# Gate/up weights of experts 2 to 15 in loads of 4 MB with rows of 32 KB, the model columns dealt out four by four, the addition of the expert outputs placed among the gate/up chunks, another seating of the first experts' weights, and the fourth norm in eight banks

## What is computed

```python
def expert_choice_ffn(h, w_router, w_gate, w_up, w_down):
    ...
    top_w, top_idx = lax.top_k(affinity.transpose(0, 2, 1), cap)   # cap = 64 of 512 tokens
    xe = jax.vmap(lambda hb, ib: hb[ib])(h, top_idx)
    hid = jax.nn.silu(jnp.einsum('becd,edf->becf', xe, w_gate)) * jnp.einsum('becd,edf->becf', xe, w_up)
    ye = jnp.einsum('becf,efd->becd', hid, w_down) * top_w[..., None].astype(h.dtype)
    combine = lambda yb, ib: jnp.zeros((S, D), h.dtype).at[ib.reshape(-1)].add(yb.reshape(-1, D))
    ...
# second block, its last part
h = h + swiglu(rmsnorm(h, g_ffn[l]), w_gate[l], w_up[l], w_down[l])
```

## Time and profile before

| | |
|---|---|
| time, median of 3 runs | 2044.65 us (2042.44 to 2046.21) |
| the profiled execution | 2044.67 us, of which the span is 2042.9 us |
| PE / PEld busy | 1902.7 us (93%) / 1124.7 us (55%) |
| DVE / ACT / POOL busy | 693.0 / 466.2 / 26.9 us |
| read from memory | 510.00 MB |
| expert layer, from the first gather to the last addition | about 579 to 1507 us |

### The profile page before, as it was taken

One profiled execution on the slowest core, in us unless ns is written; L12 is line 12 of the kernel. 1 busy time (PEld: TensorE's weight loads), 2 busy tenths in 40 slices (PEclk: granted clock), 3 DMA queues, 4 the chain that ended last, 5 costly groups with the idle time before them and its releaser, 6 DMA issues.

```text
span 2042.9 us, 20340 instructions
## 1 busy us (share of the span) xinstructions
PE 1902.7 (93%) x8656; PEld 1124.7 (55%) x8656; DVE 693.0 (34%) x956; ACT 466.2 (23%) x685; POOL 26.9 (1%) x30
## 2 busy tenths in 40 slices
PE   5989989999979999999998999999999999999998
PEld 5876766556733434343433434342344578888887
DVE  6474465276321021201111121111149732222234
ACT  5347535313201101010100101010131432222223
POOL 0000000000000000000000000000030000000000
PEclk8999989999979999999999999999999999999999
DMA  8212201385579999999999999999971014332211
GB/s 306 83 42 62 62 21 42 124 309 206 236 281 422 428 427 428 427 427 428 426 429 427 428 427 428 427 428 428 416 253 53 30 49 148 104 103 84 102 62 41
DMA packets 102495, 513.41 MB, mean 251 GB/s; under 512 B 5123, under 2 KB 59523, under 8 KB 74371
## 3 DMA queue, kind: packets, MB, share of 16 engines
q1 hardware_dynamic: 98032, 487.93, 59.4%
q10 hardware_dynamic: 4374, 24.18, 3.1%
HBM read 510.00 MB, written 2.10 MB: 251 GB/s over the span
## 4 chain that ended last, share of the span: by engine, by line
PE 70%; DMA 17%; DVE 9%; ACT 3%; issue 1%; POOL 0%; SPq 0%; ACTq 0%; DVEq 0%; POOLq 0%
DMA work<-in_w_exp_up 15%; PE ps L1197 11%; PE ps L1152 10%; PE ps L1362 5%; PE ps L1321 4%; PE ps L1322 4%; PE ps L1323 4%; PE ps L600 3%; PE ps L1075 3%; PE ps L601 3%; PE ps L602 3%; PE ps L584 3%; DVE work L2382 2%; PE ps L1178 2%; PE ps L786 2%
## 5 line engine op out<-in xcount | busy, mean ns | idle before, releaser
L1152 PE MATMUL ps<-work 128*64 128x512 f32 x1280 | 451.8, 607 | 36.1 <-DMA work<-in_w_exp_up 36.1
L1152 PE MATMUL ps<-ring,work 128*64 128x512 f32 x760 | 328.4, 603 | 2.6 <-DMA ring<-in_w_exp_up 2.6
L1152 PEld LDWEIGHTS ps<-work 128*64 128x64 f32 x1280 | 141.0, 140 | 229.6 <-issue 175.0
L2295 DVE TENSOR_TENSOR stay<-stay,ps 64x512 f32<-64x512 f32 x64 | 44.3, 692 | 440.9 <-ACT stay L1734 440.3
L1734 ACT ACTIVATE stay<-ps 64x512 f32<-64x512 f32 x64 | 37.7, 589 | 555.5 <-PE ps L1152 555.5
L1152 PEld LDWEIGHTS ps<-ring,work 128*64 128x64 f32 x760 | 101.5, 139 | 113.1 <-issue 103.6
L1197 PE MATMUL ps<-work 128*64 128x512 f32 x616 | 142.0, 607 | 0.3
L584 PE MATMUL ps<-work,ring 128*128 128x512 f32 x320 | 138.7, 592 | 0.7 <-issue 0.7
L1321 PE MATMUL ps<-xh,wh 128*128 128x512 f32 x352 | 137.0, 389 | 0.0
L1322 PE MATMUL ps<-xl,wh 128*128 128x512 f32 x352 | 136.9, 389 | 0.0
L1323 PE MATMUL ps<-xh,wl 128*128 128x512 f32 x352 | 136.9, 389 | 0.0
(11 more groups left out here) (340 smaller groups left out, 2489.4 us busy)
## 6 DMA issues: line engine op xcount, KB each, us to landing
work<-in_w_exp_up SPq DMA_DIRECT2D x44, 2048.0 KB, 25.6
work<-in_w_exp_down SPq DMA_DIRECT2D x35, 2048.0 KB, 26.4
ring<-in_w_exp_gate SPq DMA_DIRECT2D x30, 2048.0 KB, 24.2
work<-in_w_exp_gate SPq DMA_DIRECT2D x29, 2048.0 KB, 23.9
ring<-in_w_exp_down SPq DMA_DIRECT2D x21, 2048.0 KB, 24.8
ring<-in_w_exp_up SPq DMA_DIRECT2D x15, 2048.0 KB, 23.4
ring<-in_w_in SPq DMA_DIRECT2D x27, 1024.0 KB, 6.7
work<-in_ada_w ACTq DMA_DIRECT2D x16, 1024.0 KB, 6.1
```

The lines of the kernel that those rows point to most:

```text
L1152: i = e.matmul(PS[64 * gu:64 * gu + 64, fb, :], at(XET + 128 * k + 64 * z, 64), weights[:, 512 * fb:512 * fb + 512], start=(k == 0), stop= ...
```

## The change

**Loads and slots.** Expert 1 keeps loads of 2 MB. For experts 2 to 14 gate and up come in four loads of 4 MB (`eg4`, `eu4`, four chunks each, rows of 32 KB) into four places of four slots each (`quads`); even and odd experts swap which two places come first. Down keeps its 2 MB loads, and goes into the two places that chunks 0 to 3 leave. Expert 15 has 4 MB loads for chunks 0 to 3, then 2 MB and 1 MB loads. The first experts' slots are dealt out in another order ("seating"): expert 0's chunk k = 2 now lies in slots 7 and 8, and expert 1's four down loads go to the pairs (7, 8), (22, 6), (4, 5), (9, 10) where they went to (7, 8), (2, 3), (4, 5), (9, 10).

**Columns.** A row of a load now holds four neighbouring columns' weights, also in the smaller loads, and `every_fourth(o, k)`, `raw(o + 512 * (k // 4) + k % 4, [(4, 128)])`, takes the place of `every_second`; the laid-out norm and router weights follow (not shown).

**Addition among the chunks.** `combine(p, tc)` does the two matmuls of one block of 128 tokens and is called behind the chunks k = 2 to 5 of an even expert; DVE's eight `add_back` come ahead of the four products of gate and up.

**Fourth norm.** The transposes use all eight banks, token block by token block, without waiting for `sx_l`; ACT and DVE read `bank(k)`. The dense groups u = 0 and u = 1 run chunk by chunk alternately.

```diff
@@ -132,25 +132,27 @@
-    slots += [13, 14, 11, 12, 15, 16, 7, 8, 2, 3, 4, 5, 9, 10, 21, 0, 1, 19, 20, 22, 6, 13, 14, 11]
-    n = 10
-    for e in range(1, NE):
-        for kk in range(KD // 2):
-            if (e, kk) == (NE - 1, KD // 2 - 1):
-                ex += [("eg", e, 6), ("eu", e, 6), ("eg", e, 7), ("eu", e, 7)]
-                slots += [*pairs[n % 8], *pairs[(n + 1) % 8]]
-            else:
-                ex += [("eg2", e, kk), ("eu2", e, kk)]
-                slots += [pairs[n % 8], pairs[(n + 1) % 8]]
-            n += 2
-        for m in range(4):
-            if e == NE - 1:
-                ex += [("ed", e, 2 * m), ("ed", e, 2 * m + 1)]
-                slots += [*pairs[n % 8]]
-            else:
-                ex += [("ed2", e, m)]
-                slots += [pairs[n % 8]]
-            n += 1
+    slots += [13, 14, 11, 12, 7, 8, 2, 3, 4, 5, 9, 10, 21, 16, 0, 1, 22, 6, 15, 19, 20, 13, 14, 11]
+    for kk in range(KD // 2):
+        ex += [("eg2", 1, kk), ("eu2", 1, kk)]
+        slots += [pairs[(10 + 2 * kk) % 8], pairs[(11 + 2 * kk) % 8]]
+    ex += [("ed2", 1, m) for m in range(4)]
+    slots += [(7, 8), (22, 6), (4, 5), (9, 10)]
+    quads = (((0, 1), (2, 3)), ((11, 12), (13, 14)), ((22, 6), (7, 8)), ((4, 5), (9, 10)))
+    for e in range(2, NE):
+        now, then = (quads[:2], quads[2:])[::1 - 2 * (e % 2)]
+        ex += [("eg4", e, 0), ("eu4", e, 0)]
+        slots += [now[0][0] + now[0][1], now[1][0] + now[1][1]]
+        if e < NE - 1:
+            ex += [("eg4", e, 1), ("eu4", e, 1)]
+            slots += [then[0][0] + then[0][1], then[1][0] + then[1][1]]
+            ex += [("ed2", e, m) for m in range(4)]
+            slots += [*now[0], *now[1]]
+        else:
+            ex += [("eg2", e, 2), ("eu2", e, 2), ("eg", e, 6), ("eu", e, 6), ("eg", e, 7), ("eu", e, 7)]
+            slots += [*then[0], *then[1][0], *then[1][1]]
+            ex += [("ed", e, n) for n in range(8)]
+            slots += [*now[0][0], *now[0][1], *now[1][0], *now[1][1]]
     tail = [("i2", 3), ("i2", 1), ("o2", 0), ("o2", 1)] + [("i2", c) for c in (2, 0, 5, 4)] + [("o2", 2), ("o2", 3)] + [("ff", f) for f in range(33)]
...
@@ -374,11 +382,14 @@
+                r0, a0 = 512 * (key[2] // 2), 2 * (key[2] % 2)
+                return t["w_exp_gate" if kind == "eg2" else "w_exp_up"][key[1], r0:r0 + 512, :].rearrange("(p a) n -> p a n", a=4)[:, a0:a0 + 2, :]
+            if kind in ("eg4", "eu4"):
...
@@ -1085,17 +1100,18 @@
                     i = e.transpose(bank(7, 128, 128 * c), at(OHW + 128 * c, 128), ident)
                 i.then_inc(s["x_ot"], 1)
 
-            def combine(p):
-                e.wait_ge(s["x_oc"], p + 1)
-                e.wait_ge(s["x_ym"], 4 * p + 4)
-                for tc in range(TC):
-                    for dh in range(2):
-                        if tc == 0:
-
-                            e.wait_ge(s["x_hc"], 8 * p + 7 + dh)
-                        else:
-                            e.wait_ge(s["x_ca"], 8 * p + 2 * tc - 1 + dh)
-                        e.matmul(bank(6 + dh), at(OHWT + 128 * tc, 128), at(YE + 512 * dh, 512), start=True, stop=True).then_inc(s["x_cb"], 1)
+            def combine(p, tc):
+                if tc == 0:
+                    e.wait_ge(s["x_oc"], p + 1)
+                    e.wait_ge(s["x_ym"], 4 * p + 4)
+                    e.wait_ge(s["x_xd"], 4 * p + 8)
+                for dh in range(2):
+                    if tc == 0:
+
+                        e.wait_ge(s["x_hc"], 8 * p + 7 + dh)
+                    else:
+                        e.wait_ge(s["x_ca"], 8 * p + 2 * tc - 1 + dh)
+                    e.matmul(bank(6 + dh), at(OHWT + 128 * tc, 128), at(YE + 512 * dh, 512), start=True, stop=True).then_inc(s["x_cb"], 1)
 
             def combine_half(st):
                 if st == 0:
...
@@ -1154,8 +1170,9 @@
-                if z == 0 and p > 0:
-                    combine(p - 1)
+                    if z == 0 and p > 0 and 2 <= k < 6:
+                        combine(p - 1, k - 2)
+
                 if z == 1:
                     if p + 1 < NE // 2:
                         gather(p + 1)
...
@@ -1307,16 +1324,20 @@
                     p.then_inc(s["o2_pe"], 1)
 
             def t4_free(k):
-                if k < 4:
-                    e.wait_ge(s["o2_x"], (7, 8, 3, 4)[k])
-                else:
-                    e.wait_ge(s["sx_l"], SX0 + k - 3)
-            turn(XS4, [0, 1, 2, 3], lambda c: normed(4, c), t4_free, s["t_pe"])
-
-            def dense_3(bk, i, j, each=None):
-                for k in range(KD):
-                    if each is not None:
-                        each(k)
+                e.wait_ge(*((s["o2_x"], 7), (s["o2_x"], 8), (s["o2_x"], 3), (s["o2_x"], 4),
+                            (s["dv"], 4), (s["ln_a"], 1), (s["o2_x"], 5), (s["o2_x"], 6))[k])
+
+            for c in range(TC):
+                e.wait_ge(*normed(4, c))
+                for k in (2, 3, 4, 5, 6, 7, 0, 1) if c == 0 else range(KD):
+                    if c == 0:
+                        t4_free(k)
+                    i = e.transpose(bank(k, 128, 128 * c), at(XS4 + 1024 * c + 128 * k, 128), ident)
+                    if c == TC - 1:
+                        i.then_inc(s["t_pe"], 1)
+
+            def dense_3(bk, i, j, ks=range(KD)):
+                for k in ks:
                     o, x = 256 * k + 128 * j, slice(512 * k, 512 * k + 512)
                     e.matmul(bank(bk), WH[i][:, o:o + 128], XH[:, x], start=(k == 0), stop=False)
                     e.matmul(bank(bk), WH[i][:, o:o + 128], XL[:, x], start=False, stop=False)
...
@@ -1330,12 +1351,20 @@
                         u = 4 * n + 2 * gu + j
                         if j == 0:
                             e.wait_ge(s["fs_l"], FS0 + f + 1)
-                        if u < 4:
-
-                            e.wait_ge(s["sx_l"], SX0 + 5 + u)
-                        else:
+                        if u == 0:
+
+                            for k in range(KD):
+                                e.wait_ge(s["sx_l"], SX0 + k + 1)
+                                p = dense_3(0, 0, 0, [k])
+                                if k > 0:
+                                    dense_3(1, 0, 1, [k - 1])
+                            p.then_inc(s["ff_pe"], 1)
+                            dense_3(1, 0, 1, [KD - 1]).then_inc(s["ff_pe"], 1)
+                        if u < 2:
+                            continue
+                        if u >= 4:
                             e.wait_ge(s["ff_s" if gu == 0 else "ff_m"], 2 * n - 1 + j)
-                        dense_3(2 * gu + j, gu, j, (lambda k: e.wait_ge(s["sx_l"], SX0 + k + 1)) if u == 0 else None).then_inc(s["ff_pe"], 1)
+                        dense_3(2 * gu + j, gu, j).then_inc(s["ff_pe"], 1)
             for n in range(FT // 2):
                 i = n % 2
                 e.wait_ge(s["fs_l"], FS0 + 23 + n)
...
@@ -2289,15 +2318,13 @@
             gathered(0)
             for ex in range(NE):
                 z, p = ex % 2, ex // 2
+                if z == 0 and p > 0:
+                    for n in range(8):
+                        add_back(p - 1, n)
                 for fb in range(4):
                     e.wait_ge(s["x_sl"], 4 * ex + fb + 1)
                     sg = rows(64, 128, SG + 512 * fb, 512)
                     e.tensor_tensor(sg, sg, PS[64:128, fb, :], ALU.mult).then_inc(s["x_hd"], 1)
-                    if z == 0 and p > 0:
-                        add_back(p - 1, fb)
-                if z == 0 and p > 0:
-                    for n in range(4, 8):
-                        add_back(p - 1, n)
                 if z == 1 and p + 1 < NE // 2:
                     gathered(p + 1)
                 if ex == NE - 1:
```

More of the change, by code:

```diff
@@ L218, in build @@
         parts = []
-        for name, start, end in (("stay", 0, HEAD), ("ring", HEAD, WORK), ("work", WORK, AR)):
+        for name, start, end in (("stay", 0, HEAD), ("ring", HEAD, SLOT[4]), ("work", SLOT[4], AR)):
             parts.append((start, end, nc.alloc_sbuf_tensor_at(name, [128, end - start], F32, offset=BASE + 4 * start)))
@@ L401, in rooms_of @@
                 return flat(key)
-            if kind in ("eg2", "eu2", "ed2"):
+            if kind in ("eg2", "eu2"):
+                return twice(key).rearrange("p (a n) -> p a n", a=2)
+            if kind in ("eg4", "eu4"):
+                return four(key)
+            if kind == "ed2":
                 return twice(key)
@@ L436, in last_reader @@
                 return s["wo_pe"], 4 * (key[1] // 2) + 4
[L437 to L438 removed]
+            if kind in ("eg", "eu", "eg2", "eu2", "eg4", "eu4"):
+                k = key[2] if len(kind) == 2 else 2 * key[2] + 1 if kind[2] == "2" else 4 * key[2] + 3
                 return s["x_gu"], 18 * key[1] + (18 if k == KD - 1 else 2 * k + (1 if kind[:2] == "eg" else 2))
```

38 lines of the change are left out of this document (20 added, 18 removed).

## The result

The changed kernel takes 2138.55 us (median of 4 runs, 2136.41 to 2141.7); the kernel before, timed beside it, 2043.55. The ratio is 1.0464, with a 95% interval of 1.0452 to 1.0476: 95 us slower, where 9.4 were predicted and 2062 was the upper end of the range. The direction was right, the size was not. The profiled execution took 2136.41 us, its span is 2134.6.

The account below looks back on a forecast made before the run. The prediction took the streaming of expert weights as the bound up to expert 14's last up load, then TensorE alone. 2044.67 + 11.8 (end of the expert layer) - 2.5 (fourth norm) = 2054.0 us, range 2043 to 2062.

Parts of the forecast that it names:

- The column step: Reading columns four apart instead of two: the same instructions with another step, so 0; bounds nothing and 37 us.
- the four places: Six expert pairs: down loads wait for chunks 0 to 3 and come late; +6.1 us, ends 3.5 and 9.5.
- the addition among the chunks: Even experts' addition inside gate/up: worth 0 by itself, hidden by transfers; without it the four places would starve at each.
- the second rival: Gather in odd experts: reads with a step of four floats take twice the time; 2091 us in all, 4 in 100.
- The longer rows: 54 loads of 4 MB with 32 KB rows save 0.073 us each; -4.0 us, ends 0 and -8.0.
- Expert 1's down loads: The second down load waits for chunk 5 of expert 1 and lands at 662.3 instead of 657.7; +4.6 us.
- they must be issued 2.7 us ahead: Even experts' down loads: issued 2.7 us before the queue's owed transfers end, they keep it full.
- The clock: TensorE behind longer waits for 4 MB loads: a slow stretch in six of ten; 1.0 us at expert 15.
- The end of the layer: Expert 15 starts behind a wait at 1462.0; its gate/up ends at 1491.2, 11.8 us later than 1479.35.
- The fourth norm: With eight banks and two groups by turns, TensorE starts the dense groups at 1673.9; -2.5 us, ends -1.5 and -2.8.

Follow-up runs that it names:

- Experiment 1: The changed kernel with columns read two apart instead of four (weights meet other columns than their own): 2081.33 us, ratio 1.0174.
- experiment 5: The changed kernel with rows of 16 KB in its 4 MB loads and columns two by two: 2078.80 us, ratio 1.0181.
- experiment 10: The changed kernel with 16 KB rows, columns two by two, addition behind gate/up, and expert 1's down loads with (22, 6) last: 2062.31 us, ratio 1.0098.
- experiment 11: The changed kernel with 32 KB rows, columns read two apart, addition behind gate/up, and expert 1's down loads with (22, 6) last: 2063.82 us, ratio 1.0097.
- experiment 8: The kernel of experiment 1 with expert 1's down loads in the order (7, 8), (4, 5), (9, 10), (22, 6): 2076.36 us, ratio 1.0171.
- experiment 2: The kernel before with columns read four apart instead of two, nothing else changed: 2059.72 us, ratio 1.0073.
- experiment 6: The kernel of experiment 1 with the addition of even experts back behind gate/up: 2067.34 us, ratio 1.0123.
- experiment 7: The kernel before with the addition of even experts among their chunks, nothing else changed: 2044.37 us, ratio 1.0003.
- experiment 3: The kernel before with only the change's fourth norm: 2041.76 us, ratio 0.9986.
- the fifth expectation: The text written ahead of experiment 5; its rival had the 16 engines end a 4 MB load up to 1.2 us apart. Measured: 2078.80 us.
- experiment 4: The kernel before with another column step in each expert pair's gather, stationary 1 to 8 floats, once moving 4; only the gathers' times count, 7.4 to 15.5 us.
- experiment 9: The kernel before with further stationary and moving steps in each pair's gather, up to 32 floats; only gather times count, both operands at four 15.38 us.

## Why the prediction was wrong, step by step

Three steps failed. The column step, put at nothing, is 57 of the 84.6 us. In the other 27 are the four places, with the lead that their loads need (some 23 us against 6.1 less 4.0 for the rows), and the addition among the chunks (10 to 14 against 0); the parts were measured in different kernels and do not add exactly.

**"Nothing for the columns four by four: the same instructions, with another step."** This step failed, and with it the weight of the second rival. The instructions are the same, but each pass of the gather takes 15.15 / 64 = 0.237 us instead of 0.121. The argument against the rival compared the gather's passes with transposes that read without a step. In the changed kernel the second norm's transposes read with a step of four, and still follow each other every 0.12 us, as they did with two: so a step of four does not show on them, and they could say nothing of the gather. The trace of before had no step over two, both bounds were written down, and I chose between them by a row that did not bear on it.

**The rival's own price, 37 us, was too low.** Experiment 1 against the changed kernel gives 57. The rival had 7.2 us a pair; it is 130.3 - 122.3 = 8.0 (first pairs), and it left out what lies ahead of expert 3. There the single-column matmuls of the second modulation read with a step of four as well (16 of them 3.5 us instead of 1.8, twice), and the two parts of the gather that lie at expert 0 take 2.3 and 2.8 longer: gate/up of expert 0 starts at 593.4 instead of 586.5, that of expert 2 at 704.5 instead of 687.5.

**The longer rows, -4.0.** Right in the price (9.72 predicted, 9.71 to 9.72 measured), worth nothing in the time (experiments 5 against 1, 10 against 11). That a queue which keeps running dry does not profit from rate is a likely reason, not shown by itself.

**Expert 1's down loads, +4.6.** The mechanism is there: issued at 664.38 behind chunk 5, with the queue dry since 660.5, landed 8.2 us later (7.6 predicted). The queue lost 7.2 us there (6.4 in experiment 1), not 4.6, since it was dry for longer; but part comes back behind it. Its price in the whole is 3.5 to 5 by the medians of experiments 8 and 11, and 0.6 and 5 by their ratios, so not well resolved.

**The four places, +6.1.** Mis-sized. Experiment 11, free of the step, the addition and the gap at expert 1, is 20.3 us over the kernel before, though it has the fourth norm's gain: some 23 for loads of 4 MB into four places. Of these 6.5 are a gap at expert 2 that the prediction did not look at: its second gate load waits until expert 1's down has freed a place, and goes out at 687.9 into a queue dry since 685.2. In the pairs the step that failed is the lead, "they must be issued 2.7 us ahead". That was the price of a start into an empty queue, taken as what a running queue needs. The changed kernel's first down load of expert 3 shows it. It was issued at 779.8, when the load ahead had until 783.2:

```profile
L589 SPq DMA_DIRECT2D work<-in_w_exp_down x1: 327/327/327, 779.8 to 779.8; - x1
...
DMA to landing us min/median/max: 10.3/10.3/10.3
```

It landed at 790.1, not at 783.2 + 4.9 = 788.1, in spite of 3.4 us of lead. Over all expert loads of 2 and 4 MB issued behind 648 us in nine kernels (before, after, experiments 1, 2, 5, 6, 8, 10, 11), with the lead as the landing of the load ahead minus the own issue:

```
lead, us    loads   late by over 0.3   median loss, us
under 1        25          25              4.1
1 to 2         13          13              1.6
2 to 3         38          36              1.8
3 to 4         58          43              0.9
4 to 5         49          17              0.1
5 to 6         50          10              0.1
6 to 8         94           7              0.0
over 8        775          31              0.0
```

So about 6 us of lead are needed for a loss to be rare. The prediction's own leads were 3.2 us at the down loads (1.5 behind a slow stretch) and 2.3 at the next gate load. With experiment 11's leads behind 730 us the prediction's rule, 2.7 less the lead, gives 0.3 us in all, and the queue lost 20.0 (6 in the kernel before); in experiment 1 the rule gives 10.9 of 37.2. The rest of the miss is TensorE, which came later than the sums had it (43.3 against 39.8).

**The clock.** I took six in ten of the longer waits to bring a slow stretch. In the changed kernel all do. Behind the six waits of 6.0 to 7.0 us for the first pair of the experts 3 to 13, 64 passes take 16.3 to 16.9 us, against 13.73 at full clock. Behind the seven waits for the last up load of these experts and the first of expert 15, 62 passes take 15.35 to 16.86 us, against the 13.95 that 62 such passes take in experiment 10 at a granted clock of 1.00. Six of these seven waits are 2.6 to 3.1 us long, no longer than before; the prediction had 4 to 5.7. The window behind the one in expert 3:

```profile
783.30:786.50 3.20, 3.20 (x8) 0.99 (x10) 0.00 (x0) 0.00 (x0) 0.00 (x0) 0.50 0.90 343
```

Of the Trainium skill ("TensorE: Matmul & The Clock Gate", section "HAM oscillation — how this bites in real kernels") it is the rule, weighed in the prediction and set aside in favour of the count over shorter waits, that was borne out in this kernel. It is not so everywhere: in experiment 10, 4 of 13 waits (3.1 to 3.4 us) left the passes at full clock.

**The addition among chunks, 0.** Right for the kernel before (experiment 7), wrong in this one: 10 to 14 us (experiment 6). "Without it the place above would starve" had the sign reversed. It looked at when TensorE finishes, not at when chunk 3 and chunk 7 are read: each block of 1.9 us ahead of a chunk is a block of delay for the loads that wait for its place.

**The end of the layer.** Expert 15 stood behind the wait as foretold, but at 1542.9 instead of 1462, by all of the above. **The fourth norm, -2.5:** right (2.6 in the trace, 2.5 in experiment 3).

Still open is why a load issued 3 to 4 us ahead loses in three of four cases and not in the fourth. Row length is excluded by experiment 5. The traces hold a part of the answer: a load's semaphore counts sixteen completions, one an engine, and over the same loads the first and the last of the load ahead lie 2.4 us apart (median; the fifth expectation had up to 1.2 for a 4 MB load). Where the lead to the last was 3 to 4 us, the first engine was done only 1.2 us behind the issue (median), so it may have stood idle until the new load reached it. But this is alike for the loads that lost and for those that did not (1.2 and 1.3), so it does not tell them apart.

## What to carry to other kernels

A layout that makes a load's rows longer is paid for where the data are read: look at the step of every operand that follows from it, above all in matmuls with 128 columns whose stationary or moving data are float32, and if no row shows that step in that kind of instruction, measure it first. Fewer and larger loads into the same places take away lead, and lead is what hid the other delays here: the step of four cost 15 us in the kernel whose loads leave early and 57 in the one whose loads leave late, and the addition among the chunks cost nothing in the one and 10 to 14 in the other. Ask of each work that is moved in among reads whose place it keeps from coming free.

## What the runs showed of the chip beyond that

A 128 x 128 float32 matmul pass takes 0.115 us with a step of one, 0.121 with two, 0.178 with three and 0.222 to 0.241 with 4, 5, 6, 7, 8, 16 and 32 floats, for the stationary operand (64 passes of experiments 4 and 9); the moving operand is the same within 5% at 2, 3 and 4, and the two do not add (0.240 with four on both). The second norm's float32 transposes do not slow down with a step of four: 0.12 us each.

Slow operand reads were followed by a lower clock, without any wait. In the changed kernel the 16 single-column matmuls at 479.4 to 482.8 run at 1.00, and the matmuls behind them at 0.50, the lower level of 1.2 GHz; windows:

```profile
479.40:482.80 3.40, 3.40 (x16) 3.40 (x17) 1.34 (x2) 0.00 (x0) 0.00 (x0) 1.00 0.00 0
482.90:486.30 3.40, 3.40 (x9) 2.66 (x9) 3.37 (x3) 1.91 (x1) 0.00 (x0) 0.50 0.00 0
```

In the kernel before the same matmuls take 1.8 us, and what follows stays at full clock:

```profile
481.40:483.20 1.80, 1.80 (x18) 1.80 (x17) 1.38 (x2) 0.00 (x0) 0.00 (x0) 1.00 0.00 0
483.30:486.60 3.30, 3.30 (x16) 2.69 (x16) 3.26 (x3) 1.88 (x1) 0.00 (x0) 1.00 0.00 0
```

The step alone does this too: in the kernel before with a step of four (experiment 2) the 16 matmuls take 3.5 us and the clock falls behind them, and in the changed kernel with a step of two (experiment 1) they take 1.8 and it stays at 1.00. Experiment 2:

```profile
485.20:488.10 2.90, 2.90 (x8) 2.33 (x7) 2.87 (x2) 1.50 (x1) 0.00 (x0) 0.50 0.00 0
```

PE counts as busy throughout in all these windows, so the busy share does not tell of the fall; the granted clock does.
